# Prompt attentions: ScalarE copies the turned probabilities of three steps back before its own step's exponential, not behind it

## What is computed

```
# forgetting attention, per head, causal
logits = q @ k.T * scale + cum_q[:, None] - cum_k[None, :]
p = masked_softmax(logits, k_pos <= q_pos)
o = p @ v
# sparse attention, per query head: the same softmax over three key sets
o = g[0] * o_cmp + g[1] * o_sel + g[2] * o_win
```

## Time and profile before

| | |
|---|---|
| median of 3 runs | 2777.14 us (2760.77 to 2780.5) |
| profiled execution: its own time | 2772.47 us |
| span in the profile | 2770.8 us |
| PE busy, share of the span | 82% |
| DVE, ACT busy | 43%, 21% |
| granted TensorE clock, mean | 0.89 |
| forgetting attention of the prompt, start to end | about 311 to 373 us |
| sparse attention of the prompt, start to end | about 1409 to 1682 us |

### The profile page before, as it was taken

The page is one execution under the profiler, slowest core; times in us unless marked ns, Lnnn a source line. Parts: engine busy times, 40 slices in busy tenths (PEclk is TensorE's granted clock), DMA queues, the critical chain, the costliest instruction groups (busy, mean ns, idle before and its releaser), DMA issues. The chain is left out here.

```text
span 2770.8 us, 46037 instructions
## 1 busy us (share of the span) xinstructions
PE 2269.3 (82%) x16993; PEld 1961.9 (71%) x16993; DVE 1202.7 (43%) x2134; ACT 581.4 (21%) x999; POOL 270.4 (10%) x433
## 2 busy tenths in 40 slices
PE   3983546776999898896669896999997766999898
PEld 2862432355999898793468785777885456999898
DVE  4314721135444432425355554556543345444432
ACT  2101111002111000201125354445441212111000
POOL 0010223300000000000012122112110310000000
PEclk7995778788999999897679798999998998999999
DMA  6651059962223221223200004223233841233221
GB/s 254 217 195 44 0 197 386 384 249 96 84 83 91 87 85 57 69 69 140 95 1 1 1 1 126 88 92 122 71 113 139 308 143 54 86 89 86 91 96 56
DMA packets 238575, 321.92 MB, mean 116 GB/s; under 512 B 17851, under 2 KB 196104, under 8 KB 230959
## 3 DMA queue, kind: packets, MB, share of 16 engines
q1 hardware_dynamic: 211671, 199.44, 22.1%
q0 software_dynamic: 26720, 120.09, 11.8%
HBM read 311.56 MB, written 16.42 MB: 118 GB/s over the span
## 5 line engine op out<-in xcount | busy, mean ns | idle before, releaser
L381 PE MATMUL ps<-XHup,WHup 128*128 128x272 f32 x1408 | 293.4, 290 | 28.8 <-DVE XLup L357 25.3
L381 PE MATMUL ps<-XHup,WLup 128*128 128x272 f32 x1408 | 292.9, 290 | 0.0
L381 PE MATMUL ps<-XLup,WHup 128*128 128x272 f32 x1408 | 291.8, 289 | 0.0
L381 PEld LDWEIGHTS ps<-XHup,WHup 128*128 128x128 f32 x1408 | 223.1, 190 | 30.8 <-DVE XLup L357 26.8
L1954 PE MATMUL ps<-CHi,W1H 128*128 128x512 f32 (+1 forms) x512 | 207.5, 405 | 19.6 <-DVE CLo L2023 19.6
L381 PEld LDWEIGHTS ps<-XLup,WHup 128*128 128x128 f32 x1408 | 222.8, 190 | 0.0
L381 PEld LDWEIGHTS ps<-XHup,WLup 128*128 128x128 f32 x1408 | 221.3, 190 | 0.0
L2023 DVE TENSOR_TENSOR CLo<-RAWc,CHi 128x512 fp32r<-128x512 f32 x128 | 139.8, 1113 | 163.4 <-ACT CHi L1977 163.4
L1955 PE MATMUL ps<-CLo,W1H 128*128 128x512 f32 (+1 forms) x512 | 205.6, 402 | 0.0
L1956 PE MATMUL ps<-CHi,W1L 128*128 128x512 f32 (+1 forms) x512 | 204.7, 400 | 0.0
L1977 ACT CAST CHi<-RAWc 128x512 fp32r<-128x512 f32 x128 | 143.1, 1155 | 155.4 <-PE ps L1956 136.0
(11 more groups left out here) (458 smaller groups left out, 4163.4 us busy)
## 6 DMA issues: line engine op xcount, KB each, us to landing
RAWup<-in_w_up SPq DMA_DIRECT2D x88, 512.0 KB, 3.9
Wmod<-in_w_mod POOLq DMA_DIRECT2D x20, 2048.0 KB, 10.7
VP<-in_cache_fox_v POOLq DMA_DIRECT2D x128, 256.0 KB, 6.0
KP<-in_cache_fox_k SPq DMA_DIRECT2D x128, 256.0 KB, 10.4
RAWdn<-in_w_down SPq DMA_DIRECT2D x14, 1408.0 KB, 6.4
RAWin<-in_nsa_w_in SPq DMA_DIRECT2D x20, 512.0 KB, 3.6
KS<-in_cache_nsa_ks SPq DMA_DIRECT2D x80, 128.0 KB, 2.9
Wmod<-in_w_mod SPq DMA_DIRECT2D x4, 2048.0 KB, 19.1
```

The costliest lines, as they stand in the source:

```text
L381: mm = self.nc.tensor.matmul(self.ps[:, banks + n, 0:HALF], w, x[:, n * HALF:(n + 1) * HALF], start=start, stop=stop)
```

## The change

ACT's step is written in another order: the copy of unit s-3 stands first, and the exponential of unit s (or the copy of the turned output) behind it. Nothing else is changed, neither waits nor counts nor buffers; the instructions of the other engines are the same. In the changed kernel the dense copy is L1237, the compressed one L1241, the exponential L1248 and the copy of the output L1252.

```diff
             @block.scalar
             def _(act):
                 for step in range(steps):
-                    kind, n = items[step] if step < len(items) else (None, None)
-                    if kind == "unit":
-                        w = width(*units[n])
-                        act.wait_ge(sems["maxima"], n + 1)
-                        if n >= 4:
-                            act.wait_ge(sems["turned"], n - 3)
-                        nc.scalar.activation(P3[:, n % 4, 0:w], ps[:, made[step] % S_BANKS, 0:w], ACT.Exp,
-                                             bias=NM[:, n:n + 1]).then_inc(sems["bank_read"], 1)
-                    elif kind == "out":
-                        act.wait_ge(sems["scores"], made[step] + 1)
-                        nc.scalar.copy(outs[n], ps[:, made[step] % S_BANKS, :]).then_inc(sems["bank_read"], 1)
                     n = unit_of(step, COPY)
                     if n is not None and not by_dve[n]:
                         g, i = units[n]
...
                         else:
                             w = width(g, i)
                             nc.scalar.copy(PC[0:w, n % 3, :], ps[0:w, T_BANK + n % 2, 0:P]).then_inc(sems["out_act"], 1)
+                    kind, n = items[step] if step < len(items) else (None, None)
+                    if kind == "unit":
...
```

More of the change, by code:

```diff
@@ L1252, in _ @@
                             nc.scalar.copy(PC[0:w, n % 3, :], ps[0:w, T_BANK + n % 2, 0:P]).then_inc(sems["out_act"], 1)
+                    kind, n = items[step] if step < len(items) else (None, None)
+                    if kind == "unit":
+                        w = width(*units[n])
+                        act.wait_ge(sems["maxima"], n + 1)
+                        if n >= 4:
+                            act.wait_ge(sems["turned"], n - 3)
+                        nc.scalar.activation(P3[:, n % 4, 0:w], ps[:, made[step] % S_BANKS, 0:w], ACT.Exp,
+                                             bias=NM[:, n:n + 1]).then_inc(sems["bank_read"], 1)
+                    elif kind == "out":
+                        act.wait_ge(sems["scores"], made[step] + 1)
+                        nc.scalar.copy(outs[n], ps[:, made[step] % S_BANKS, :]).then_inc(sems["bank_read"], 1)
             @block.vector
```

## The result

The changed kernel takes 2731.3 us (median of 6 runs, 2723.3 to 2736.8) against 2777.1 us before: ratio 0.9836, 95% interval 0.9812 to 0.9861, 46 us less. Measured again beside the last experiments it took 2729.9 us, ratio 0.9819 (0.9795 to 0.9842). I had predicted 2739.

The account below looks back on a forecast made before the run. PE was held up 46 us by copies behind exponentials; 17.2 (even periods) + 13.7 (disturbed) + 2.4 (forgetting attention) + 5 (clock) = 38 us off 2772.5 gives 2734, plus 4.7 for the median: 2739 us. Range for all cases 2710 to 2765.

Parts of the forecast that it names:

- The rival that the waits were something else: Rival: PE's waits at these places belong to the exponential, not the copies, so nothing changes: 2777 us, chance 0.06.
- waits by period: Sparse attention: PE's waits for ACT copies, 4.61 us in each of five even periods, 20.5 us in three disturbed ones.
- The even period: Undisturbed 24 units of the sparse attention, 29.7 us: net 3.44 us saved each, to 26.2; 17.2 us for five.
- give-back: New waits for late exponentials after DVE combines a group, 1.17 us of the 4.61 us removed per even period.
- the walk: Turn-by-turn reckoning of one undisturbed sparse-attention period without copy waits: 4.61 us removed, 1.17 returned, net 3.44.
- The disturbed periods: Three sparse-attention periods where DVE splits key sets: 20.5 us of copy waits less 6.8 given back, 13.7 us saved.
- 5 of clock: Sparse attention: shorter waits may keep the granted clock up longer; 5 us taken, between 0 and 20.
- The wait left at the key split: Near 1533 us, PE still stands still 2.3 of the former 4.3 us, for an exponential.
- The forgetting attention: Stage with 4.7 us of copy waits, nearer to being bound by DVE: half taken, 2.4 us, between 0 and 4.7.
- The clock's (2719 us): Rival: the clock stays up once the long waits go; gain 58 us, to 2719 us, chance 0.17.
- VectorE as the bound (2765): Rival: most turns wait for DVE's maxima instead; gain only 8 to 16 us, 2765 us, chance 0.17.
- the copy holds up the exponential: Slow-side rival: ready exponentials come later by the copy, costing 57 us against 46 saved: 2788 us, chance 0.05.

Follow-up runs that it names:

- e4: Kernel before, old ACT order, with three PSUM banks each for scores and turns, value product and combining one step later, a fourth copy buffer: 2733.1 us, ratio 0.9846.
- e5: On top of the change, VectorE splits a key set in four pieces over four steps: 2699.3 us, ratio 0.9729; measured again 2702.9 us, ratio 0.9735.
- e8: Old order on ACT, with key splits over four steps and combining over three on DVE: 2737.1 us, ratio 0.9852.
- e3: Kernel before, old ACT order, with three PSUM banks for turned probabilities and three for scores (two and four before): 2763.9 us, ratio 0.9950.

## Why the prediction was right, point by point

**What bounds.** Right. The gain is in the two stages to within a microsecond (45.5 of 45.8), and PE's copy waits were real: they fell from some 43 to 4.7 us in the sparse stage, from 4.7 to 0 in the other. The rival that the waits were something else is refuted by e4, which takes most of them away by other means and gains nearly the same. Reading start to start mattered: the idle column alone gave 27.5 us, and the sparse stage saved about 29 us of waits even after some 9 had come back.

**The sums.** The prediction's waits by period, 5 x 4.61 + 20.5, make 43.6 us, where it names 41.6 for the stage; counted over the 97 turns against free ones of 0.06 and 0.11 it is 43.2. Its new wait of 0.30 us has 2.40 and 2.15 beside it, which differ by 0.25. Neither changes the forecast. That 46 us of waits were named and 46 us were gained is chance: some 43 us of copy waits went in both stages, some 12 came back, and the rest of the gain goes with the clock.

**The even period.** Predicted 26.2 us, measured 25.85. The give-back was sized at 1.17 us and measured 0.87. Of the two places, at the one with 0.32 + 0.20 us the wait for the exponential is 0.37 and the second does not come; at the group's change the walk had 0.30 + 0.05 + 0.30 us for exponentials, and it is one wait of 0.50 us for a copy. There the walk missed that a copy now stands behind the exponential of the step before, so that a late exponential still delays a turn through it.

**The disturbed periods and the clock.** Predicted 13.7 us of waits and 5 of clock for the sparse stage, 18.7; measured 21.7 (120.3 to 98.6 us). The wait left at the key split was put at 2.3 us and is 2.7. The term that was mis-sized is the clock. Of the 40.8 us of the sparse stage, copies' waits account for some 38, less about 8 for exponentials and 1 for DVE's copy, which leaves 29. The other 12 go with some 26 us less at the lower level, where half the speed would make 13 (an estimate, as is the split). I had taken 5 of a possible 20. The Trainium skill ("TensorE: Matmul & The Clock Gate", "HAM oscillation") tells of a kernel whose long waits for data each leave the matmuls behind them at the lower clock. The long waits of this stage agree: the clock is 0.89 to 0.93 with them and 0.98 in e5. The prediction took that section for waits of any length, but it speaks of long ones, and the short ones of e8 cost nothing of the kind, 101 of them at a clock of 0.98.

**The forgetting attention.** Predicted 2.4 us, measured 4.7. Its copies' waits (4.7 us) all went, and about half came back, as predicted: turns now wait 7.0 us for exponentials and DVE's copies from start to start, 4.3 before. The other 2.7 us were in no term of the sum, which had the clock at nothing in this stage. Its granted clock rose from 0.90 to 0.92, some 9 us at the lower level for 12.5; at half the speed that makes about 2 us, an estimate.

**The rivals.** The clock's (2719 us) came true in part only, since the bursts stayed; e5, without them, has 0.98 in the sparse stage. VectorE as the bound (2765) is refuted by e5: DVE has the same work there and the two stages are 19 us shorter than with the change. That the copy holds up the exponential was seen nowhere as a cost: with the change 6 exponentials of the sparse stage start over 0.15 us after their maxima, 6 did before.

**The signs named ahead.** Stage 235 to 240 us: 232.5. Copy waits under 5 us: 3.3. Waits for exponentials 8 to 12 us: 6.3, below the range named. The even periods kept full clock. So every term came out on the low side, 19.2 for 17.2, 21.7 for 18.7 and 4.7 for 2.4 us; the mechanism holds, and the clock is the term with the largest error.

## What to carry to other kernels

Where an engine walks a hand-written order, look for work that has long been ready but stands behind an instruction with a late wait: it costs whoever waits for it, though the engine itself is idle most of the time. Take the wait from start to start, not from the idle column, and ask who needs the same result next; a further buffer at the place that the list of waits names mostly moved the wait (e3). After such a fix look at what made the late instruction late: spreading DVE's bursts over steps gave 19 us more in the two stages, for an edit that removes no work either (27 to 32 in the total, of which 10 lie in a stage that it does not touch).

## What was not expected of the hardware

When DVE splits a key set while POOL makes a split query, both get slower: in the kernel before, L1271 took 0.68 us alone (at 309.95 us, before the first scores) and 1.66 us beside POOL's L1322, whose own length there is 1.59 us where it is 1.27 in most places. L1270 just before it took 1.00 for 0.68 us. Together that is 1.3 us of the burst that held up the exponential.

A stage that no edit touches was 10 us shorter in both profiles of one kernel, at a granted clock of 0.98 to 0.99 against 0.96, and another moved by 7 us between two profiles of the same code. A difference of a per cent is safe here only with the stage it comes from.
